# Two transformer blocks on one core: rotary turns by exchanged halves, and another order of VectorE's work in the second block

## The chip, the core and the metric

The kernel runs on one core of one Trainium2 chip. TensorE (the matrix engine, PE), VectorE (DVE), ScalarE (ACT) and GpSimd (POOL) each work through a list of instructions of their own, in order; SyncE (SP) issues the loads of weights. They wait for one another through semaphores. TensorE writes its products into PSUM, eight banks of 128 partitions by 512 float32; all else lies in SBUF. The metric is the device time of one execution in microseconds (us).

## The reference

Everything is float32, with 256 tokens ("latents") of 1024 features, and 256 context tokens in the first block.

The first block has two layers. A layer normalises and modulates its input, projects it with `w_in`, forms grouped heads (6 query heads and 2 key heads of 64 features) and latent heads (6 heads of 96 features, of which the last 32 are turned), runs attention over context and latents, adds a pooling branch, projects with `w_out`, and ends with a squared-ReLU MLP of width 4096. The second block has two layers too: a projection to 10256 features, eight heads of causal attention with two maps each, eight heads of a gated recurrence computed as a second masked product, gates, and three output projections.

The part that the change touches is the rotary turn. In the first block, for the latents only:

```python
def apply_rope(x, cos, sin):
    half = x.shape[-1] // 2
    xf = x.astype(jnp.float32)
    x1, x2 = xf[..., :half], xf[..., half:]
    return jnp.concatenate([x1 * cos - x2 * sin, x1 * sin + x2 * cos], axis=-1).astype(x.dtype)
```

and the same formula for queries and keys of the second block. It is `x * cos + swapped(x) * signed_sin`, where `swapped` exchanges the two halves of a head's features. The other touched parts are the softmax of the two maps (`softmax(where(causal, q·k * scale, -inf))`, of which the kernel computes the maximum first) and `u = sigmoid(ga) * ya + sigmoid(gb) * yb; x + u @ w_o`.

## The kernel before, in words

Activations lie with features on partitions and tokens along the free axis. Weights come from HBM in slots of 1024 x 512 (2 MB) into a ring of three. Products of the MLP and of the whole second block are "split": a weight granule (1024 x 128) is rounded by ScalarE to a high part (`hi_to`, L1516), VectorE subtracts it from the raw weight to make the low part (`lo_to`, L1926), and TensorE makes three cheap products for each of eight chunks, hi·hi, hi·lo, lo·hi (`split_product`, L1128 to L1130, 24 matmuls). In the second block three granule buffers take turns, so the granule split while product n is done serves product n + 3. All other products are plain float32 matmuls.

**Units.** Queries and keys are made unit by unit (`run_units`): 4 grouped units, 6 + 6 latent ones (`qm`, `km`) in a layer of the first block, 8 + 8 units `aq`, `ak` in a layer of the second. For each unit TensorE makes the projection, ScalarE squares it (L1475), TensorE sums the squares with a matrix of ones (`mean_squares`, L1022), ScalarE makes the reciprocal root (L1486 to L1488), VectorE corrects and applies it (L1909, L1911, L1970). Four units later TensorE multiplies the unit by a constant rotation matrix (`rotate`, L1039), VectorE multiplies that by the sine table into one of two buffers `rs` (`sine_product`, L1980), and GpSimd multiplies the unit by the cosine (L892) and adds `rs` (L895); `roped` counts the units that are done. In the second block `av`, `bif` and `bv` products follow the units, before any query is used. In the first block the four `vm` products follow, and attention begins once the grouped units are turned; it reaches the latent heads after its grouped pairs.

**Steps of the second block.** There are 32 units u of (head, block of 128 queries), the first 16 of causal attention, the last 16 of the recurrence, and 37 steps. In step s TensorE transposes the weights of unit s - 2 (L1381), every second step makes an output (L1393 to L1395, into one bank that ScalarE must have emptied, L1763), makes the scores of unit s (L1410 to L1419, into two banks that ScalarE's exponentials of unit s - 1, L1748, must have emptied) and one or two of 48 further projections (`mid_of`: `first`, and `others` in 11 of 37 steps). VectorE's order in a step: the maximum of the scores (L2200), which ScalarE's exponentials wait for; `projected` for `first`, which splits the next granule (L1926) and finishes the projection (L2170, or the three convolution taps L2154); the weights of the unit (L2217 to L2219); every second step a gate (L2185); `projected` for `others`. An output's root is due in the next step, where ScalarE scales the output by it behind its exponentials (L1763); the root of the mean square is made by GpSimd in 16 small instructions (`root_of_mean`, L952 to L960).

**Output projections.** `outa`, `outb`, `wo` have eight products each. During `outb` VectorE makes `zt` (L2240), GpSimd adds it (L984), copies the sum to its high part (L985) and subtracts it for the low part (L986); `ua_ready` counts these, and VectorE waits for it before it writes `zt` again. The first `wo` product needs all eight of them, one for each of its chunks.

## Time and profile before

| | us |
|---|---|
| median of three runs | 1970.27 (1967.19 to 1971.59) |
| the profiled execution, its own time | 1969.74 |
| its span, first to last instruction | 1967.9 |

| engine | busy us | share of the span |
|---|---|---|
| PE, matmuls | 1840.9 | 94% |
| PEld, weight loads | 1477.3 | 75% |
| DVE | 1101.7 | 56% |
| ACT | 881.7 | 45% |
| POOL | 397.6 | 20% |

Busy time is a union over instructions. Ends of matmuls are modelled, so a busy TensorE need not be at its peak. The granted clock of TensorE was 0.963 of full speed over the span. An arrow in a row (`<-ACT pb L1748`) names what ended the idle time before an instruction. A matmul with float32 operands appears as two records. Layers of the first block run from about 50 to 740 us and from 740 to 1128 us, layers of the second from 1128 to 1549 us and from 1549 us to the end.

### The profile page before, as it was taken

Reading aid. Unit: us, or ns where it says so; the run is one execution under the profiler, and the core shown is the slowest. Engines: PE = TensorE matmul, PEld = TensorE weight load, DVE = VectorE, ACT = ScalarE, POOL = GpSimd, SP = SyncE. Lnnn points to the kernel's source line nnn. Section 1 sums busy time; section 2 is a strip of 40 time slices with the busy share of each in tenths; the row PEclk is TensorE's granted clock in tenths of the full one; section 3 lists DMA queues with packets and bytes.
Section 4 is the critical chain, followed back from the end, with each engine's and each line's share of the span. In section 5 each row is a group of like instructions: output and inputs, shape, how many; then the busy total and the mean of one; then the engine's idle time right before and its main releaser. Section 6 shows DMA issues by size and latency. Waiting matters only on the chain.

```text
span 1967.9 us, 28606 instructions
## 1 busy us (share of the span) xinstructions
PE 1840.9 (94%) x10840; PEld 1477.3 (75%) x10840; DVE 1101.7 (56%) x1939; ACT 881.7 (45%) x1757; POOL 397.6 (20%) x834
## 2 busy tenths in 40 slices
PE   4999999899999998999999989988999899889998
PEld 2453454588888885547999988777899898778997
DVE  3317841687777532382555576566555575655554
ACT  2327630433332324462555565555553564555542
POOL 1014200000000000230000024055544061355433
PEclk8899989899999999999899999989999999999999
DMA  8411631244555341202455534423434325322350
GB/s 302 136 45 44 213 128 43 86 171 172 187 183 187 129 110 43 86 1 73 142 173 187 194 109 147 146 87 112 142 133 172 129 98 210 127 87 92 130 199 37
DMA packets 139875, 255.26 MB, mean 130 GB/s; under 512 B 14926, under 2 KB 21724, under 8 KB 139612
## 3 DMA queue, kind: packets, MB, share of 16 engines
q1 hardware_dynamic: 138742, 251.16, 36.6%
q8 instruction: 88, 1.44, 0.3%
q0 software_dynamic: 704, 2.10, 0.3%
q14 instruction: 47, 0.39, 0.1%
q10 hardware_dynamic: 294, 0.18, 0.0%
HBM read 252.38 MB, written 1.05 MB: 129 GB/s over the span
## 4 chain that ended last, share of the span: by engine, by line
PE 80%; DVE 8%; ACT 5%; issue 3%; POOL 1%; SPq 1%; DMA 1%; ACTq 0%; DVEq 0%; POOLq 0%
PE ps L1128 16%; PE ps L1130 15%; PE ps L1129 15%; PE ps L1137 10%; PE ps L1022 3%; PE ps L1243 2%; PE ps L1269 1%; PE ps L1039 1%; PE ps L1255 1%; PE ps L1335 1%; PE ps L1336 1%; PE ps L1337 1%; PE ps L1102 1%; SPq L803 1%; DVE big_r L1926 1%
## 5 line engine op out<-in xcount | busy, mean ns | idle before, releaser
L1926 DVE TENSOR_TENSOR big_r<-ring,big_r 128x1024 fp32r<-128x1024 f32 x198 | 245.3, 1240 | 259.4 <-ACT big_r L1516 259.0
L1516 ACT ACTIVATE big_r<-ring 128x1024 fp32r<-128x1024 f32 x198 | 209.4, 1059 | 387.7 <-PE ps L1130 379.0
L1129 PE MATMUL ps<-big_r 128*128 128x256 f32 (+1 forms) x1120 | 374.4, 334 | 0.0
L1128 PE MATMUL ps<-hT_r,big_r 128*128 128x256 f32 (+1 forms) x896 | 290.9, 325 | 10.9 <-DVE big_r L1935 10.6
L1130 PE MATMUL ps<-hT_r,big_r 128*128 128x256 f32 (+1 forms) x896 | 283.5, 316 | 0.0
L1129 PEld LDWEIGHTS ps<-big_r 128*128 128x128 f32 x1120 | 215.5, 192 | 19.3
L1137 PE MATMUL ps<-hT,ring 128*128 128x512 f32 (+2 forms) x576 | 207.2, 519 | 10.8 <-ACT hT L1537 9.2
L1128 PE MATMUL ps<-big_r 128*128 128x256 f32 (+1 forms) x592 | 195.6, 330 | 1.4 <-DVE big_r L2083 1.4
L1130 PE MATMUL ps<-big_r 128*128 128x256 f32 (+1 forms) x592 | 194.6, 329 | 0.0
L1128 PEld LDWEIGHTS ps<-hT_r,big_r 128*128 128x128 f32 x896 | 172.8, 193 | 27.5 <-issue 11.8
L1137 PEld LDWEIGHTS ps<-hT,ring 128*128 128x128 f32 (+1 forms) x576 | 109.0, 191 | 105.9 <-issue 95.0
L1130 PEld LDWEIGHTS ps<-hT_r,big_r 128*128 128x128 f32 x896 | 173.2, 193 | 10.5
L1926 DVE TENSOR_TENSOR cst_r<-ring,w_ukv_sb_r 128x1024 fp32r<-128x1024 f32 x70 | 87.3, 1248 | 114.5 <-ACT w_ukv_sb_r L1516 114.5
L1128 PEld LDWEIGHTS ps<-big_r 128*128 128x128 f32 x592 | 112.4, 190 | 11.9 <-DVE big_r L2083 2.2
L1130 PEld LDWEIGHTS ps<-big_r 128*128 128x128 f32 x592 | 112.4, 190 | 10.0
L1892 DVE SCALAR_TENSOR_TENSOR pT<-ring,csilu,pT 128x512 f32<-128x512 f32 x168 | 118.5, 747 | 1.3
L1128 PE MATMUL ps<-hT_r,w_ukv_sb_r 128*128 128x256 f32 x384 | 114.6, 298 | 0.0
L1516 ACT ACTIVATE w_ukv_sb_r<-ring 128x1024 fp32r<-128x1024 f32 x70 | 74.1, 1058 | 83.6 <-PE ps L1130 72.0
L1130 PE MATMUL ps<-hT_r,cst_r 128*128 128x256 f32 x384 | 110.0, 286 | 0.0
L1129 PE MATMUL ps<-xT_r,w_ukv_sb_r 128*128 128x256 f32 x384 | 109.8, 286 | 0.0
L907 POOL MEMSET big<- 128x1088 f32 x2 | 2.2, 1080 | 531.3 <-PE ps L1130 531.3
L1909 DVE SCALAR_TENSOR_TENSOR nt<-ps,nt 128x256 f32<-128x256 f32 (+3 forms) x74 | 39.0, 527 | 125.9 <-ACT nt L1488 125.6
(290 smaller groups left out, 4144.0 us busy)
## 6 DMA issues: line engine op xcount, KB each, us to landing
ring<-in_w_in SPq DMA_DIRECT2D x42, 2048.0 KB, 7.8
ring<-in_w_mlp SPq DMA_DIRECT2D x32, 2048.0 KB, 7.8
ring<-in_w_mod SPq DMA_DIRECT2D x24, 2048.0 KB, 8.0
ring<-in_w_out SPq DMA_DIRECT2D x4, 2048.0 KB, 8.5
ring<-in_w_out_a SPq DMA_DIRECT2D x4, 2048.0 KB, 8.6
ring<-in_w_out_b SPq DMA_DIRECT2D x4, 2048.0 KB, 8.0
ring<-in_w_o SPq DMA_DIRECT2D x4, 2048.0 KB, 8.5
ring<-in_w_in SPq DMA_DIRECT2D x12, 256.0 KB, 5.1
```

Source lines behind the costliest of these rows:

```text
L803: queue.dma_start(prow[row:row + src.shape[0], s, off:off + src.shape[1]], src).then_inc(rows_landed[s], 16)
L1022: last = mm(b[0:parts, 0:T], ones, sq[0:parts, n % SQ, 0:T], start=(j == 0), stop=(j == chunks - 1))
L1039: fill(mm(b[0:parts, 0:SEQ], rot, lat, start=True, stop=True), key)
L1128: mm(b[:, 0:T], w_hi[:, k, :], hi(k), start=(k == 0), stop=False)
L1129: mm(b[:, 0:T], w_hi[:, k, :], lo(k), start=False, stop=False)
L1130: last = mm(b[:, 0:T], w_lo[:, k, :], hi(k), start=False, stop=(k == KC - 1))
L1137: last = mm(b[0:cols, 0:T], w[:, k, m:m + cols], src(k), start=(k == 0), stop=(k == KC - 1))
L1243: fill(mm(banks[e][:, 0:tiles * P], lhs, rhs, start=True, stop=True), (tag, "s", 2 * j + e))
L1516: act_fn(hi, raw, ACT.Copy).then_inc(hi_ready, 1)
L1892: ins = V.scalar_tensor_tensor(acc, w, c, acc, ALU.mult, ALU.add)
L1909: drain(V.scalar_tensor_tensor(r2, bank(key)[0:parts, 0:T], width * EPS, r2, ALU.add, ALU.mult), key)
L1926: V.tensor_tensor(lo, raw, hi.bitcast(F32), ALU.subtract).then_inc(lo_ready, 1)
```

## The change

It has three parts.

1. The rotation products, their banks and the two rotation matrices are gone. Units are turned in four groups a layer ("turns"): 2, 2, 6 and 6 units in the first block, 4 each in the second. When the last unit of a turn is in SBUF, GpSimd issues DMAs that copy each half to the other half's partitions in a free buffer (4 DMAs, or 2 for the latent heads, whose 32 rows alone take part); GpSimd multiplies all units of the turn by the cosine in one instruction, VectorE the swapped copy by a signed sine in one instruction, and GpSimd adds them. VectorE's instruction stands two units after the turn's last one, for the fourth turn after the granules of `av` (second block) or in step 2 of attention (first block). The scores of the second block wait once for all four turns.
2. In the steps of the second block, VectorE puts the last `projected` of each step behind the next step's maximum.
3. During `outb`, GpSimd only adds; ScalarE makes the high part (`u_rounded`) and VectorE the low part (`u_rest`), and VectorE splits its granule after `zt` instead of before.

The diff, cut to its core; the removed `rope_units`, `rotate` and `sine_product` are printed above.

```diff
@@ constants
 MS_LAG = 1
-ROT_LAG = 4
+SWAP_LAG = 2
+SWAP_STEP = 2
-    put("rot64", P, rotation(P, [(0, 32), (64, 32)]))
-    put("rot96", MQK, rotation(MQK, [(MNOPE, MROPE // 2)]))
+    put("sign", P, np.where(np.arange(P) % HD < HD // 2, -1.0, 1.0)[:, None])
-    put("sing", P, np.tile(sg, (4, 1)))
+    put("sing", P, np.concatenate([-sg, sg, -sg, sg], 0))
-    put("sinm", MQK, np.concatenate([np.zeros((MNOPE, SEQ)), sm, sm], 0))
+    put("sinm", MQK, np.concatenate([np.zeros((MNOPE, SEQ)), -sm, sm], 0))
+def turns_of(tag):
+    if tag[0] == "b":
+        return [[f"a{x}{c}" for c in range(n, n + 4)] for x in "qk" for n in (0, 4)]
+    return [["q0", "q1"], ["q2", "k"], [f"qm{h}" for h in range(MH)], [f"km{h}" for h in range(MH)]]
+        def turn_of(tag, t):
+            if tag[0] == "b":
+                units = (aqT, akT)[t // 2][:, 4 * (t % 2):4 * (t % 2) + 4, :]
+                return units, pT[:, 0, :, :], cos2[:, :], sin2[:, :], slice(0, P), HD // 2
+            if t < 2:
+                units = big[:, 0:4 * TOK].rearrange("p (c t) -> p c t", c=4)[:, 2 * t:2 * t + 2, LAT:]
+                return units, rs[:, :, :], cc("cosg"), cc("sing"), slice(0, P), HD // 2
+            units = (qmT, kmT)[t - 2][:, :, LAT:]
+            free = hT[:, 3:6, :].rearrange("p c (s t) -> p (c s) t", s=2)
+            return units, free, cc("cosm"), cc("sinm"), slice(MNOPE, MQK), MROPE // 2
+        def turned(tag, t):
+            return 4 * ((DEPTH if tag[0] == "b" else 0) + tag[1]) + t + 1
@@ POOL
-            def rope_units(tag, units, part):
...
+            def turn(tag, t):
+                units, free, cos, _, rows, half = turn_of(tag, t)
+                for name in turns_of(tag)[t]:
+                    await_drained(pool, (tag, name, 0))
+                for o in range(rows.start, rows.stop, 2 * half):
+                    for to, of in ((o, o + half), (o + half, o)):
+                        pool.dma_start(free[to:to + half, :, :], units[of:of + half, :, :]).then_inc(swap_landed, 16)
+                        swaps[0] += 16
+                pool.wait_ge(swap_landed, swaps[0])
+                x = units[rows, :, :]
+                link(nc.gpsimd.tensor_tensor(x, x, cos[rows, :].unsqueeze(1).to_broadcast(list(x.shape)), ALU.mult))
+                pool.wait_ge(sine_made, turned(tag, t))
+                nc.gpsimd.tensor_tensor(x, x, free[rows, :, :], ALU.add).then_inc(roped, 1)
+                pool.wait_ge(roped, turned(tag, t))
-                rope_units(tag, units_a(i), 0)
-                rope_units(tag, units_m(i), 1)
+                for t in range(4):
+                    turn(tag, t)
-                rope_units(tag, units_b(), 0)
+                for t in range(4):
+                    turn(tag, t)
-                    link(nc.gpsimd.tensor_tensor(tgaT[:, c, :], tgaT[:, c, :], zt[:, c % 2, :], ALU.add))
-                    link(nc.gpsimd.tensor_copy(u_hi[:, c, :], tgaT[:, c, :]))
-                    nc.gpsimd.tensor_tensor(u_lo[:, c, :], tgaT[:, c, :], u_hi[:, c, :].bitcast(F32), ALU.subtract)\
-                        .then_inc(ua_ready, 1)
+                    nc.gpsimd.tensor_tensor(tgaT[:, c, :], tgaT[:, c, :], zt[:, c % 2, :], ALU.add).then_inc(u_summed, 1)
@@ TensorE
-            def rotate(tag, name):
-                for j in range(n + ROT_LAG):
+                for j in range(n + max(MS_LAG, len(tail))):
-                    if 0 <= j - ROT_LAG and is_roped(units[j - ROT_LAG][0]):
-                        rotate(tag, units[j - ROT_LAG][0])
-                pe.wait_ge(roped, roped_before(tag, 1))
+                pe.wait_ge(roped, turned(tag, 1))
-                            pe.wait_ge(roped, roped_before(tag, 1) + 2 * MH)
+                            pe.wait_ge(roped, turned(tag, 3))
                 for step in range(STEPS):
+                    if step == 0:
+                        pe.wait_ge(roped, turned(tag, 3))
-                        if p < NH2:
-                            pe.wait_ge(roped, roped_before(tag, 0) + NH2 + h + 1)
-                        else:
+                        if p >= NH2:
@@ ScalarE
+                def u_rounded(c):
+                    act.wait_ge(u_summed, 8 * l + c + 1)
+                    act_fn(u_hi[:, c, :], tgaT[:, c, :], ACT.Copy).then_inc(u_hi_ready, 1)
                     hi_to(split_by((tag, name, c)))
+                    if name == "outb" and c >= 1:
+                        u_rounded(c - 1)
+                    if name == "outb" and c == 7:
+                        u_rounded(c)
@@ VectorE
-            def sine_product(tag, name):
+            def sine_product(tag, t):
+                _, free, _, sin, rows, half = turn_of(tag, t)
+                n_swaps[0] += 16 * (rows.stop - rows.start) // half
+                dve.wait_ge(swap_landed, n_swaps[0])
+                x = free[rows, :, :]
+                V.tensor_tensor(x, x, sin[rows, :].unsqueeze(1).to_broadcast(list(x.shape)), ALU.mult)\
+                    .then_inc(sine_made, 1)
             def run_units(tag, units):
+                names = [name for name, _, _ in units]
+                at = {names.index(turn[-1]) + SWAP_LAG: t for t, turn in enumerate(turns_of(tag)[:3])}
                 for j, (name, kind, _) in enumerate(units):
...
+                    if j in at:
+                        sine_product(tag, at[j])
                 if tag[0] == "b":
                     lo_to(gran_no[("av", tag[1], 0), 3] + B_BUFS)
+                    sine_product(tag, 3)
@@ VectorE, attention of the first block
                     if j < steps:
+                        if j == SWAP_STEP:
+                            sine_product(tag, 3)
@@ VectorE, steps of the second block
+                left = []
                 for step in range(STEPS):
...
                         V.tensor_reduce(st[:, 2:4], scores, AX_X, ALU.max, negate=True).then_inc(nmax_ready, 1)
+                    for name, c in left:
+                        projected(name, c)
+                    left = (first + others)[-1:]
...
-                    for name, c in first:
+                    for name, c in (first + others)[:-1]:
                         projected(name, c)
...
-                    for name, c in others:
-                        projected(name, c)
+                for name, c in left:
+                    projected(name, c)
...
+                def u_rest(c):
+                    dve.wait_ge(u_hi_ready, 8 * l + c + 1)
+                    V.tensor_tensor(u_lo[:, c, :], tgaT[:, c, :], u_hi[:, c, :].bitcast(F32), ALU.subtract)\
+                        .then_inc(ua_ready, 1)
                 for c in range(8):
                     key = (tag, "outb", c)
                     await_bank(dve, key)
-                    lo_to(split_by(key))
-                        dve.wait_ge(ua_ready, 8 * l + c - 1)
+                        dve.wait_ge(u_summed, 8 * l + c - 1)
...
+                    lo_to(split_by(key))
+                    if c >= 1:
+                        u_rest(c - 1)
+                u_rest(7)
```

## Rows read from the trace of the kernel before

**Rows 1.** The page, the chain that ended last: shares of the span by engine.

```profile
PE 80%; DVE 8%; ACT 5%; issue 3%; POOL 1%; SPq 1%; DMA 1%; ACTq 0%; DVEq 0%; POOLq 0%
```

**Rows 2.** Stretches: length, busy PE, PEld, DVE, ACT, POOL, granted clock, DMA share, GB/s.

```profile
1256.90:1355.80 98.90, 82.58 (x643) 75.13 (x642) 60.52 (x112) 55.37 (x166) 44.39 (x108) 0.94 0.31 113
1363.00:1447.50 84.50, 84.50 (x638) 75.74 (x637) 46.32 (x117) 44.27 (x117) 41.63 (x142) 1.00 0.34 118
1670.40:1770.50 100.10, 84.30 (x644) 76.80 (x643) 60.77 (x112) 55.59 (x166) 43.56 (x108) 0.93 0.31 112
```

**Rows 3.** Timeline of TensorE, second block's units: start us, us, instruction, records.

```profile
1170.38 0.59 PE L1039 MATMUL ps<-big,cst 128*128 128x256 f32 x2
1170.81 0.38 PE L1022 MATMUL ps<-sq,cst 128*128 128x256 f32 x1
...
1174.08 0.59 PE L1039 MATMUL ps<-big,cst 128*128 128x256 f32 x2
...
1174.76 0.47 PE L1128 MATMUL ps<-hT_r 128*128 128x256 f32 x1
```

**Rows 4.** Stretches of four units (second block) and three `km` units (first).

```profile
1160.10:1175.00 14.90, 14.90 (x114) 14.48 (x113) 12.25 (x22) 10.17 (x21) 9.80 (x9) 1.00 0.41 142
170.10:180.40 10.30, 10.30 (x25) 2.68 (x24) 8.41 (x12) 7.50 (x13) 4.07 (x7) 1.00 0.01 2
```

**Rows 5.** Timelines of VectorE and GpSimd in those units of the second block.

```profile
1168.02 1.22 DVE L1926 TENSOR_TENSOR hT_r<-ring,hT_r 128x1024 fp32r<-128x1024 f32 x1 [0.31 <-ACT hT_r L1516]
1171.01 0.42 DVE L1980 TENSOR_TENSOR rs<-ps,sin 128x256 f32<-128x256 f32 x1
1171.75 1.23 DVE L1926 TENSOR_TENSOR big_r<-ring,big_r 128x1024 fp32r<-128x1024 f32 x1 [0.32 <-ACT big_r L1516]
1171.86 1.71 POOL L895 TENSOR_TENSOR big<-big,rs 128x256 f32<-128x256 f32 x1
```

**Rows 6.** Groups by line and shape of GpSimd.

```profile
L881 POOL DMA_DIRECT2D w_pool_sb<-in_w_pool x8 | 4.2, 526 | 0.0
L915 POOL TENSOR_TENSOR big<-big 128x542 f32<-128x542 f32 x2 | 2.2, 1088 | 0.0
L915 POOL TENSOR_TENSOR big<-big 128x271 f32<-128x271 f32 x2 | 1.3, 637 | 0.0
```

**Rows 7.** DMA issues: engine, number, KB each, median us to landing.

```profile
w_pool_sb<-in_w_pool POOLq DMA_DIRECT2D x8, 16.0 KB, 7.7
out<-ring SPq DMA_DIRECT2D x1, 1024.0 KB, 4.0
```

**Rows 8.** Timelines around one stall in the second block's steps.

```profile
1300.18 0.20 POOL L960 TENSOR_TENSOR rn<-rn,stat 128x2 f32<-128x2 f32 x1
1302.20 2.36 DVE L2154 SCALAR_TENSOR_TENSOR big<-sq,prm,big 128x256 f32<-128x256 f32 x3
1304.49 0.68 DVE L2200 TENSOR_REDUCE stat<-ps 128x2 f32<-128x512 f32 x1
1306.85 0.52 PE L1393 MATMUL ps<-big,pT 128*128 128x128 f32 x2 [3.89 <-ACT sq L1763]
1310.48 0.25 POOL L952 TENSOR_SCALAR rn<-rn 128x2 f32<-128x2 f32 x1
1315.78 0.44 POOL L960 TENSOR_TENSOR rn<-rn,stat 128x2 f32<-128x2 f32 x1
```

**Rows 9.** TensorE's waits, first and third stretch of Rows 2: us, times, longest.

```profile
PE ps L1393 <- ACT sq L1763: 8.7, 3, 3.9
PE ps L1410 <- ACT pb L1748: 7.1, 5, 2.8
...
PE ps L1393 <- ACT sq L1763: 8.9, 3, 3.8
```

**Rows 10.** TensorE's timeline, first `wo` product of each layer.

```profile
1519.87 0.39 PE L1128 MATMUL ps<-big_r,w_ukv_sb_r 128*128 128x256 f32 x1 [1.02 <-POOL xT_r L986]
1521.82 0.39 PE L1128 MATMUL ps<-big_r,w_ukv_sb_r 128*128 128x256 f32 x1 [1.33 <-POOL xT_r L986]
```

More of the change, by code:

```diff
@@ L75 @@
 _at = 0
-for _name, _n in (("ident", P), ("ones", P), ("ones64", P), ("rot64", P), ("rot96", MQK), ("mask", P),
+for _name, _n in (("ident", P), ("ones", P), ("ones64", P), ("mask", P), ("sign", 1),
                   ("invf", 1), ("cosg", SEQ), ("sing", SEQ), ("cosm", SEQ), ("sinm", SEQ), ("invn", 2 * SEQ)):
@@ L93, in shape_constants @@
     put("ones64", P, np.kron(np.eye(2), np.ones((64, 64))))
-    def rotation(n, blocks):
-        r = np.zeros((n, n))
-        for s, half in blocks:
-            for j in range(half):
-                r[s + half + j, s + j] = -1.0
-                r[s + j, s + half + j] = 1.0
-        return r
-    put("rot64", P, rotation(P, [(0, 32), (64, 32)]))
-    put("rot96", MQK, rotation(MQK, [(MNOPE, MROPE // 2)]))
     put("mask", P, np.where(np.arange(P)[None, :] > np.arange(P)[:, None], -1e30, 0.0))
+    put("sign", P, np.where(np.arange(P) % HD < HD // 2, -1.0, 1.0)[:, None])
     put("invf", P, (np.float32(THETA) ** (-np.arange(0, HD, 2, dtype=np.float32) / np.float32(HD)))
@@ L209, in unit_plan @@
                 ms += 1
-                if is_roped(name):
-                    take((tag, name, "rot"), 6 + rot % 2)
-                    rot += 1
     for i in range(DEPTH):
@@ L882, in _ @@
             pool.wait_ge(const_landed, 32)
-            def rope_units(tag, units, part):
-                n = roped_before(tag, part)
-                for name, kind, _ in units:
-                    if kind != "norm" or not is_roped(name):
-                        continue
-                    parts, t0, T, dsts, _, _, _, (_, cos, _) = unit_of(tag, name)
-                    lat = dsts[0] if tag[0] == "b" else dsts[0][:, LAT - t0:]
-                    await_bank(pool, (tag, name, "rot"))
-                    link(nc.gpsimd.tensor_tensor(lat, lat, cos[0:parts, :], ALU.mult))
-                    await_drained(pool, (tag, name, "rot"))
-                    nc.gpsimd.tensor_tensor(lat, lat, rs[0:parts, n % 2, :], ALU.add).then_inc(roped, 1)
-                    n += 1
+            swaps = [0]
+            def turn(tag, t):
[12 more added lines that the diff above has]
+                pool.wait_ge(roped, turned(tag, t))
             for i in range(DEPTH):
@@ L1777, in _ @@
                         projected(name, c)
-                for key in [(tag, name, c) for name in AFTER for c in range(8)]:
-                    await_bank(act, key)
-                    hi_to(split_by(key))
+                for name, c in [(name, c) for name in AFTER for c in range(8)]:
+                    await_bank(act, (tag, name, c))
+                    hi_to(split_by((tag, name, c)))
+                    if name == "outb" and c >= 1:
+                        u_rounded(c - 1)
+                    if name == "outb" and c == 7:
+                        u_rounded(c)
         @block.vector
@@ L1961, in _ @@
             nt_free = []
-            n_rot = [0]
             def apply_norm(tag, name):
-                parts, t0, T, dsts, gains, _, width, _ = unit_of(tag, name)
+                parts, t0, T, dsts, gains, _, width = unit_of(tag, name)
                 n = newton((tag, name, "ms"), parts, T, width)
@@ L1990, in run_units @@
                         apply_norm(tag, name)
-                    pend.append(name if is_roped(name) else None)
-                    if len(pend) > 2 and pend[-3]:
-                        sine_product(tag, pend[-3])
+                    if j in at:
+                        sine_product(tag, at[j])
                 if tag[0] == "b":
                     lo_to(gran_no[("av", tag[1], 0), 3] + B_BUFS)
-                for name in pend[-2:]:
-                    if name:
-                        sine_product(tag, name)
+                    sine_product(tag, 3)
             def residual(key, m, i, gate, s0):
```

55 lines of the change are left out of this document (17 added, 38 removed).

## The prediction

> **What bounds the kernel now.** I read the page's chain first. TensorE carries 80% of the path that ended last, VectorE 8%, ScalarE 5% [rows 1]: time is won where TensorE loses an instruction that it executes, a wait, or half its clock, and hardly anywhere else. So the next view is the table of stretches, set over the steps of the second block. From step 0 to step 15 of the first of its layers 98.9 us pass with TensorE busy for 82.58, at a granted clock of 0.94; the same number of steps and of projections (20) in the recurrence half take 84.5 us, without idle, at 1.00. The second layer shows 100.1 us, 84.30 busy, 0.93 [rows 2]. Here lies most of what is to be had: 16.3 + 15.8 = 32.1 us idle, and 0.06 x 98.9 + 0.07 x 100.1 = 12.9 us of clock, since the levels are 1.2 and 2.4 GHz and the mean falls after the idle times. The waits name two causes, L1410 behind ScalarE's exponentials and L1393 behind ScalarE's scaling L1763 [rows 9].
>
> In the units TensorE has no gap, so each rotation counts in full: L1039 starts at 1170.38, the next instruction at 1170.81, and the next L1039 at 1174.08, that is 0.43 us in a unit of 3.70 [rows 3].
>
> **Part 1, the turns.** Removed from TensorE: 16 rotations a layer, 64 in all, at 0.43 us.
> Second block: 32 x 0.43 = 13.8 us, if nothing else becomes late. A unit then takes 3.27 us and a turn of four 13.1. VectorE is busy for 12.25 us in four units now [rows 4]; four sine products of 0.42 go, one of 1024 columns with both inputs in SBUF comes, for which I take the 1.23 us of L1926, the same shape [rows 5]: 11.8 of 13.1, 1.3 to spare. GpSimd now has four DMA issues at 0.53 = 2.1 us [rows 6], then the landing, then two instructions of 1024 columns. Those show nowhere; 271 columns take 0.64 and 542 take 1.09 us [rows 6], so 1.66 ns a column and 1.9 us on that line; in proportion to the shorter one it would be 2.4. I take 2.0. The landing shows nowhere either: 1 MB into an idle memory landed in 4.0 us, 16 KB issued by GpSimd beside other loads in 7.7 [rows 7]. A turn moves 0.5 MB; between weight loads that take 0.41 of the DMA engines [rows 4] I take the 4.0, nearest in size, and keep both ends. Then the swap is there 6.1 us after the turn's last unit, and VectorE asks for it two units on, 6.5 us: just in time. GpSimd's turn is 2.1 + 4.0 + 2 x 2.0 = 10.1 of 13.1 us, so turns don't queue up. At 7.7 VectorE waits 3.3 us.
> By the Trainium skill ("DMA: Bandwidth & Descriptors", Anatomy of one DMA) a DMA from GpSimd costs about 2.0 us plus bytes over 436 GB/s; an estimate by that page is 3.2 us for the turn, earlier than the value I use, and no row here shows such a copy.
> What hides a delay of VectorE: the granule split at 1168.02 to 1169.24 is used at 1174.76 [rows 5, 3], a lead of 5.5 us, 4.7 once two rotations less lie between. Queued behind the waiting sine product are the next units' newton steps and granules.
> A new cost is the shared access to SBUF. GpSimd's L895 starts 0.11 us behind VectorE's L1926 (1171.75, 1.23 us) and takes 1.71 us [rows 5], though 271 columns take it 0.64 [rows 6]: it ran only when VectorE was through. Now GpSimd's instructions are the long ones: two of 2.0 us a turn, each of which can hold a granule's subtraction. Bounds 0 and 4 us a turn; I take 2 us, 0.7 over the 1.3 to spare, so about 2 us a layer at most once the lead is eaten, 1 us taken. **Gain 12 us.**
> The Trainium skill ("SBUF — State Buffer", Who interferes with whom) says that the port pair goes to one of them for a whole instruction, and that two SBUF inputs on VectorE suffice for it; by that rule the trace agrees, and with splitting costing nothing the sum would be 1 or 2 us better.
> First block: 32 rotations. Eight lie among the `vm` products, where TensorE waits for VectorE anyway: 24 x 0.43 = 10.3 us. Behind the last `km` unit VectorE loses sine products and gains one of 1536 columns (1.8 us, twice, one of them in attention's step 2); GpSimd's of 1536 columns take 2.7 us on the same line, and VectorE, busy for 8.41 of 10.3 us in three `km` units [rows 4], has 0.6 us a unit to make that good. Bounds -4 to +4 us for both layers; I take -0.3. Attention's grouped pairs don't need the latent turns; these end some 12 us after the last unit, before the six steps of grouped pairs do. **Gain 10 us.**
>
> **Part 2, the maximum ahead.** One stall shows it all. VectorE is in L2154 from 1302.20, makes the maximum L2200 only at 1304.49, ScalarE's exponentials and then L1763 follow, and L1393 starts at 1306.85 after 3.89 us idle. GpSimd's root had been ready since 1300.38 [rows 8]: the maximum was late, not the root, though the wait reads L1763. With the maximum in front it starts with the scores, a granule (1.23) and sometimes a convolution (2.36 there) earlier, and the exponentials end within TensorE's projection of 24 x 0.12 = 2.9 us. So the L1410 waits go (7.1 us here, about as much in the next layer), and the L1393 waits as far as the maximum caused them (8.7 + 8.9) [rows 9].
> What is late next is the root's chain. An output starts at 1306.85; GpSimd begins at 1310.48 (its queue held a silu) and ends at 1316.22 [rows 8]; with L1763's 0.6 the next output can start 10.0 us on. TensorE's two steps take 84.5 / 15 x 2 = 11.3 us on average [rows 2] with 2.7 projections, but 9.4 with two; there 0.6 us stays idle, in about three pairs a layer, more when GpSimd is held by a granule. I leave a third of the L1393 waits. The new wait: behind the maximum stands the deferred granule. It waits for scores that TensorE makes right after the product whose bank frees that granule, at most 1.9 us, against two projections (5.7 us) until it is needed: hidden. For the recurrence half the order is the same but for the gate: nothing.
> Sum: 14 + 2/3 x 17.6 + 2/3 x 12.9 (clock, as the idle times that it follows go) = **34 us**; bounds 18 and 45.
>
> **Part 3, the rounding shared.** In the first `wo` product TensorE waits 1.02 and 1.33 us for GpSimd's last chunks [rows 10]; the other layer has somewhat more, and both a half-clock stretch behind. Afterwards the last chunk needs `zt`, an add (0.73), a copy on ScalarE behind its granule (1.06), a subtraction on VectorE behind its granule: about 3.3 us after the last `outb` product, 1.7 us earlier than now. ScalarE and VectorE have room in a product of 2.8 us (1.5 and 2.1). 2 x 1.7 + 1.6 of clock = **5 us**, bounds 2 and 10.
>
> Sum against the profiled execution, 1969.7 us: 12 + 10 + 34 + 5 = 61, **1909 us**. That execution stands 0.5 us under the median of three runs.
>
> **Rivals.**
> A. The swap is late or GpSimd's long instructions hold VectorE: landing 7.7, 3.3 us waited in three turns a layer, and 4 us a turn blocked. Against the lead of 4.7 and 1.3 a turn that leaves TensorE idle for most of what the rotations gave in the second block (12) and half in the first (5), with some 4 us of clock: 1930. For it: L895's 1.71, and 7.7. Against: the 7.7 belong to small copies queued behind larger ones of the same engine.
> B. The root's chain takes the place of the maximum and the steps win only half, 17: 1926. For it: 10.0 against 9.4 us; against: in the stall shown the root had been ready for 4.1 us when the maximum began [rows 8], and the recurrence half shows the same chain with no idle at all [rows 2].
> C. Slower. GpSimd cannot issue while VectorE holds the port: each issue waits a granule, 4 x (0.53 + 1.23) = 7.0, plus 7.7 to land, and a turn is 14.7 + 4.0 = 18.7 us against 13.1. The third sine product comes 19 us late; less 4.7 and 3 x 1.3 that is 11 us a layer, 22. In the first block two latent turns each come 5 us late in both layers, 20. Clock at 0.4 us per idle us, as in the stretches (12.9 / 32.1), 17; half of GpSimd's 16 x 2.2 us in VectorE's way, 17. Together 76 on 1909: 1985. It decides from a turn of 13.1 us on, and beats the gains from a loss of 61. Against: issues at 0.53 are short, the engine is idle between.
> The Trainium skill ("SBUF — State Buffer", SBUF: two separate sides) warns that GpSimd cannot write descriptors while VectorE is in a 2-port mode; VectorE's instructions here are mostly of two inputs, at one column a cycle, and no issue in this trace lies beside one, so it raises C's chance only a little.
> D. All idle time and clock of the named places come back: 45 + 13.8 + 12 + 8 = 79, 1891.
>
> **Chances.** Forecast 0.42 (1899 to 1919), A 0.20, B 0.20, D 0.10, C 0.06, and 0.02 that gains and losses meet. The range takes in D, A and B: 1890 to 1942. A measurement of this kernel tells 0.2% (4 us) from nothing: faster 0.92, same 0.02, slower 0.06.
>
> **What would show it.** Right: in the steps of causal attention no wait of L1410, L2200 within 0.1 us of the scores, granted clock 0.98 or more, the stretch at 80 to 84 us; a unit of 3.3 us in the second block; sine products of 1.2 us with at most 0.5 idle in front; no wait on GpSimd in the first `wo` product. Wrong: TensorE waiting for L1926 in the units, GpSimd's turn above 13 us, VectorE idle for the swap by 3 us (A, C), or L1393 waiting for L1763 right behind L960 (B).

## The result and the profile after

The changed kernel is slower by 0.3%: 1974.7 us median (1969.4 to 1983.9, 20 runs) against 1970.3 (1967.2 to 1972.4, 20 runs), ratio 1.0028, 95% interval 1.0018 to 1.0037. The forecast was 1909, its range 1890 to 1942. The profiled execution took 1975.4 us, its span is 1973.5. Line numbers have moved: the granule's L1926 is L1922 in the kernel after, the steps of the root L1909, L1911 and L1970 are L1905, L1907 and L1965, TensorE's L1022, L1128 and L1393 are L1021, L1116 and L1383, and ScalarE's L1763 is L1755; the kernels of the experiments move them again by a few lines. The page of after, engines and chain:

```profile
PE 1826.4 (93%) x10712; PEld 1457.1 (74%) x10712; DVE 1138.9 (58%) x1907; ACT 888.4 (45%) x1773; POOL 374.7 (19%) x762
...
PE 77%; DVE 9%; ACT 4%; DMA 3%; POOL 3%; issue 2%; SPq 1%; ACTq 0%; DVEq 0%; POOLq 0%
PE ps L1116 16%; PE ps L1118 15%; PE ps L1117 15%; PE ps L1125 10%; PE ps L1021 3%; DMA pT<-big 2%; PE ps L1231 2%; PE ps L1257 1%; DVE rstd L1907 1%; PE ps L1243 1%; DVE big_r L1922 1%; PE ps L1090 1%; PE ps L1323 1%; SPq L801 1%; PE ps L1324 1%
```

Compared with [rows 1], DMA and GpSimd have gone from 1% to 3% of the path each, and the path names the swap (`DMA pT<-big`) and VectorE's L1907 and L1922. TensorE is busy for 14.5 us less and the span is 5.6 us longer. To see where, I cut both traces at the same points of the work (the first score, the first product of a kind) and compared the lengths:

| stretch, us | before | after | difference |
|---|---|---|---|
| start to the end of the first block | 1129.2 | 1135.3 | +6.1 |
| units, two layers | 61.1, 60.4 | 71.7, 71.5 | +21.7 |
| `av`, then to step 0 | 56.1, 54.5 | 60.6, 61.4 | +11.4 |
| steps 0 to 16 | 106.1, 106.7 | 90.5, 92.0 | -30.3 |
| steps 16 to 31 | 84.8, 84.8 | 87.6, 87.6 | +5.6 |
| step 31 to the next layer, to the output | 96.7, 98.4 | 93.3, 93.2 | -8.6 |

The turns cost 39 us where 22 were to be won; parts 2 and 3 win 33 where 39 were forecast. Stretches of after (columns as in [rows 2]); the first and third answer to the first and third there, the second to its second, the fourth is the units, the last the output projections:

```profile
1278.20:1360.50 82.30, 77.26 (x642) 70.99 (x641) 59.24 (x111) 55.74 (x166) 46.13 (x104) 1.00 0.36 126
1368.70:1456.30 87.60, 87.60 (x638) 78.61 (x638) 46.01 (x114) 44.17 (x116) 40.74 (x143) 0.96 0.33 116
1693.20:1777.00 83.80, 78.81 (x642) 72.30 (x641) 59.55 (x111) 55.96 (x166) 46.41 (x104) 0.98 0.36 126
1146.00:1217.60 71.60, 61.77 (x414) 58.23 (x415) 54.26 (x75) 42.55 (x83) 21.64 (x17) 0.86 0.40 119
...
1456.30:1549.60 93.30, 91.92 (x771) 90.91 (x769) 52.13 (x76) 39.56 (x64) 19.89 (x48) 1.00 0.52 185
```

The units of before, for the fourth:

```profile
1139.80:1200.80 61.00, 61.00 (x438) 58.67 (x439) 48.36 (x84) 40.62 (x80) 26.79 (x22) 0.94 0.33 113
```

In the units TensorE now idles for 9.8 us and its mean granted clock is 0.86 instead of 0.94. Two turns show why. GpSimd in the second block's units (start, duration, instruction, idle before and who ended it):

```profile
1179.33 3.42 POOL L894 TENSOR_TENSOR big<-big,cos 128x1024 f32<-128x1024 f32 x1 [6.75 <-DMA pT<-big]
1182.83 3.21 POOL L896 TENSOR_TENSOR big<-big,pT 128x1024 f32<-128x1024 f32 x1
...
1209.83 2.00 POOL L890 DMA_DIRECT2D pT<-big  x4 [3.83 <-DVE big L1965]
1214.33 2.37 POOL L894 TENSOR_TENSOR big<-big,cos 128x1024 f32<-128x1024 f32 x1 [2.50 <-DMA pT<-big]
```

VectorE, an undisturbed unit first, then beside GpSimd's first two instructions above, last beside the L894 at 1214.33:

```profile
1171.81 0.42 DVE L1905 SCALAR_TENSOR_TENSOR nt<-ps,nt 128x256 f32<-128x256 f32 x1 [0.31 <-ACT nt L1476]
...
1172.72 0.48 DVE L1965 SCALAR_TENSOR_TENSOR big<-ps,prm,rstd 128x256 f32<-128x256 f32 x1
...
1179.28 1.23 DVE L1975 TENSOR_TENSOR pT<-pT,sin 128x1024 f32<-128x1024 f32 x1 [2.76 <-DMA pT<-big]
1180.42 3.42 DVE L1922 TENSOR_TENSOR big_r<-ring,big_r 128x1024 fp32r<-128x1024 f32 x1
...
1184.20 2.12 DVE L1907 SCALAR_TENSOR_TENSOR rstd<-nt,rstd 128x256 f32<-128x256 f32 x1
1186.36 0.48 DVE L1965 SCALAR_TENSOR_TENSOR big<-ps,prm,rstd 128x256 f32<-128x256 f32 x1
...
1215.22 1.75 DVE L1907 SCALAR_TENSOR_TENSOR rstd<-nt,rstd 128x256 f32<-128x256 f32 x1
```

TensorE in the same stretch:

```profile
1175.51 0.59 PE L1021 MATMUL ps<-sq,cst 128*128 128x256 f32 x2
1175.75 0.47 PE L1116 MATMUL ps<-hT_r,w_ukv_sb_r 128*128 128x256 f32 x1
...
1184.22 1.22 PE L1021 MATMUL ps<-sq,cst 128*128 128x256 f32 x2 [1.99 <-DVE nt L1905]
1186.89 0.58 PE L1116 MATMUL ps<-hT_r,big_r 128*128 128x256 f32 x1 [1.45 <-DVE big L1965]
```

Three delays follow one another. VectorE waits 2.76 us for the swap. Its granule L1922 then takes 3.42 us instead of 1.22, beside L894, which had begun 1.1 us before it. L1907, 0.42 us undisturbed, takes 2.12 beside L896. The ends of the rows show the two engines taking turns, instruction by instruction: L1975 ends at 1180.51, L894 2.24 us later, L1922 1.09 us after that, L896 2.20 us after L1922, L1907 0.28 us after L896. So each duration is a wait for the other engine's instruction and then its own time, and GpSimd's own time is 2.2 us, not 3.4. Not every instruction is held: L1905, which takes one of its inputs from PSUM, took 0.41 us at 1183.76, in the middle of L896. At 1214.33 L894 got in with hardly a wait, took 2.37 us, and it was L1907 that waited (1.75). TensorE idles for 3.4 us in the first of these turns, and the products behind run at half the clock (L1021 takes 1.22 us for its 0.59; granted clock 0.50 from 1187 to 1190).

The first block shows the same: GpSimd, then VectorE with its 96-row units, then GpSimd, VectorE and TensorE in attention, where the instruction that is held is the scaling of the attention weights, L2039:

```profile
170.11 2.90 POOL L894 TENSOR_TENSOR big<-big,cst 32x1536 f32<-32x1536 f32 x1 [2.33 <-DMA hT<-big]
176.26 3.42 POOL L896 TENSOR_TENSOR big<-big,hT 32x1536 f32<-32x1536 f32 x1 [3.25 <-DVE hT L1975]
```

```profile
170.61 2.95 DVE L1907 SCALAR_TENSOR_TENSOR rstd<-nt,rstd 96x512 f32<-96x512 f32 x1
...
176.88 3.36 DVE L1907 SCALAR_TENSOR_TENSOR rstd<-nt,rstd 96x512 f32<-96x512 f32 x1
181.65 0.69 DVE L1907 SCALAR_TENSOR_TENSOR rstd<-nt,rstd 96x512 f32<-96x512 f32 x1
```

```profile
192.72 2.90 POOL L894 TENSOR_TENSOR big<-big,cst 32x1536 f32<-32x1536 f32 x1 [2.36 <-DMA hT<-big]
198.16 3.41 POOL L896 TENSOR_TENSOR big<-big,hT 32x1536 f32<-32x1536 f32 x1 [2.54 <-DVE hT L1975]
```

```profile
192.71 3.06 DVE L2039 TENSOR_SCALAR pb<-pb,stat 128x256 f32<-128x256 f32 x1
195.88 0.35 DVE L2039 TENSOR_SCALAR pb<-pb,stat 128x256 f32<-128x256 f32 x1
199.56 2.15 DVE L2039 TENSOR_SCALAR pb<-pb,stat 128x256 f32<-128x256 f32 x1
```

```profile
201.87 0.66 PE L1243 MATMUL ps<-cst,pb 128*128 128x128 f32 x2 [4.02 <-DVE pb L2039]
```

### The profile page after: what moved, and what is told of

It reads as the page before. It is cut to its first block, busy times and chain, and to the rows that moved or that the text cites. A ratio compares the mean times of both kernels' runs of the same rounds, so it can differ in the third digit from the quotient of the medians.

```text
span 1973.5 us, 28119 instructions
## 1 busy us (share of the span) xinstructions
PE 1826.4 (93%) x10712; PEld 1457.1 (74%) x10712; DVE 1138.9 (58%) x1907; ACT 888.4 (45%) x1773; POOL 374.7 (19%) x762
## 4 chain that ended last, share of the span: by engine, by line
PE 77%; DVE 9%; ACT 4%; DMA 3%; POOL 3%; issue 2%; SPq 1%; ACTq 0%; DVEq 0%; POOLq 0%
PE ps L1116 16%; PE ps L1118 15%; PE ps L1117 15%; PE ps L1125 10%; PE ps L1021 3%; DMA pT<-big 2%; PE ps L1231 2%; PE ps L1257 1%; DVE rstd L1907 1%; PE ps L1243 1%; DVE big_r L1922 1%; PE ps L1090 1%; PE ps L1323 1%; SPq L801 1%; PE ps L1324 1%
## 5 line engine op out<-in xcount | busy, mean ns | idle before, releaser
L1922 DVE TENSOR_TENSOR big_r<-ring,big_r 128x1024 fp32r<-128x1024 f32 x198 | 252.4, 1275 | 234.7 <-ACT big_r L1504 234.7
L1116 PE MATMUL ps<-hT_r,big_r 128*128 128x256 f32 (+1 forms) x896 | 293.7, 328 | 16.5 <-DVE big_r L1931 12.8
L1116 PEld LDWEIGHTS ps<-hT_r,big_r 128*128 128x128 f32 x896 | 176.3, 197 | 33.4 <-issue 11.8
L1116 PE MATMUL ps<-big_r 128*128 128x256 f32 (+1 forms) x592 | 195.6, 330 | 1.4 <-DVE big_r L2078 1.4
L1125 PEld LDWEIGHTS ps<-hT,ring 128*128 128x128 f32 (+1 forms) x576 | 108.4, 190 | 106.7 <-issue 96.0
L1118 PEld LDWEIGHTS ps<-hT_r,big_r 128*128 128x128 f32 x896 | 176.5, 197 | 10.2
L1922 DVE TENSOR_TENSOR cst_r<-ring,w_ukv_sb_r 128x1024 fp32r<-128x1024 f32 x70 | 95.0, 1357 | 81.4 <-ACT w_ukv_sb_r L1504 81.4
L1905 DVE SCALAR_TENSOR_TENSOR nt<-ps,nt 128x256 f32<-128x256 f32 (+3 forms) x74 | 38.9, 526 | 152.2 <-ACT nt L1476 151.5
L1116 PEld LDWEIGHTS ps<-big_r 128*128 128x128 f32 x592 | 112.5, 190 | 11.9 <-DVE big_r L2078 2.2
L1116 PE MATMUL ps<-hT_r,w_ukv_sb_r 128*128 128x256 f32 x384 | 114.2, 297 | 3.3 <-DVE big L1965 3.3
L1021 PE MATMUL ps<-sq,cst 128*128 128x256 f32 (+3 forms) x236 | 90.2, 494 | 19.3 <-DVE nt L1905 9.9
```

Of the source, the lines that this page charges most:

```text
L1021: last = mm(b[0:parts, 0:T], ones, sq[0:parts, n % SQ, 0:T], start=(j == 0), stop=(j == chunks - 1))
L1116: mm(b[:, 0:T], w_hi[:, k, :], hi(k), start=(k == 0), stop=False)
L1118: last = mm(b[:, 0:T], w_lo[:, k, :], hi(k), start=False, stop=(k == KC - 1))
L1125: last = mm(b[0:cols, 0:T], w[:, k, m:m + cols], src(k), start=(k == 0), stop=(k == KC - 1))
L1905: drain(V.scalar_tensor_tensor(r2, bank(key)[0:parts, 0:T], width * EPS, r2, ALU.add, ALU.mult), key)
L1922: V.tensor_tensor(lo, raw, hi.bitcast(F32), ALU.subtract).then_inc(lo_ready, 1)
```

## Experiments

Each kernel ran 4 times beside 7 runs of the kernel before. Ratios are to the kernel before, with their 95% interval.

**1. The parts one by one.** `turns_only` is the kernel before with part 1, `ahead_only` with part 2, `rest_only` with parts 2 and 3; the edits are those of the diff above.

> The kernel before with part 1 alone. Theory L: the first block loses 6 us and the units, av and the wait at step 0 of the second block 33 us, as in the changed kernel, so 1970 + 39 = 2009 us. Rival S: the turns delay the start of the steps but the steps then run with less idle time, so that a part comes back: 1990 us.

> The kernel before with parts 2 and 3 of the change alone (maximum ahead, rounding shared); the rotation products stay. Theory L (the turns lost time by themselves, and parts 2 and 3 won it): the stretches of the steps and of the output projections moved by -24.7 and -8.6 us in the changed kernel, so this one takes 1970 - 33 = 1937 us, with the units at 61 us as before. Rival S (the gain of the steps was borrowed: the turns delayed the start of the steps, so that granules and loads of weights were further ahead when they began): step 0 to 16 wins less than half of its 15 us, and the time is 1950 or more.

> The kernel before with part 2 alone. By the stretches steps 0 to 31 won 24.7 us in the changed kernel and the output projections 8.6: so 1970 - 25 = 1945 us, and part 3 is worth 7 (1938.7 for both). Forecast in the prediction: 34 for part 2 and 5 for part 3, that is 1936 here. Rival: the two hang together (the output projections also win by the order of the granules at the end of the steps), 1940.

| kernel | us | ratio |
|---|---|---|
| part 1 | 2010.2 | 1.020 (1.0171 to 1.0230) |
| part 2 | 1947.8 | 0.9888 (0.9873 to 0.9904) |
| parts 2 and 3 | 1938.7 | 0.9840 (0.9822 to 0.9858) |

Theory L holds, rival S falls: the turns lose 38 us by themselves, and with rotation products in front of them steps 0 to 31 still win 22.5 of the 24.7 us. Part 2 is worth 23 us, part 3 another 9, the difference of two ratios that are each uncertain by 3 to 4 us. In what follows 1938.7 is the mark that a kernel with turns must beat.

**2. GpSimd's instructions in unit pieces** (`cut`).

```diff
-link(tensor_tensor(x, x, cos[...].to_broadcast(...), mult))      # all units of the turn
+for k in range(n): tensor_tensor(units[rows, k, :], units[rows, k, :], cos[rows, :], mult)
-tensor_tensor(x, x, free[rows, :, :], add)
+for k in range(n): tensor_tensor(units[rows, k, :], units[rows, k, :], free[rows, k, :], add)
```

> The changed kernel with GpSimd's two instructions of a turn cut into one for each unit (4 x 256 columns in the second block, 6 x 256 rows-by-columns for the latent heads), all else the same. Theory P (a long GpSimd instruction holds VectorE for its whole length): VectorE waits for at most one piece of some 0.8 us at a time, L1922 and L1907 in the units fall from 3.4 and 2.1 us to at most 2 and 1.2, the units of the second block go from 71.6 to about 65 us a layer and attention in the first block back to its 95.6 and 45.7: together 1975 - 2 x 6 - 10 = 1953 us. Rival Q (what counts is the late swap, 6.9 us to land against 4.0): the pieces change nothing in the wait for the swap, and the time stays at 1970 to 1978.

1953.1 us, 0.9910 (0.9893 to 0.9927). GpSimd and VectorE in one turn:

```profile
1168.83 5.99 POOL L896 TENSOR_TENSOR big<-big,cos 128x256 f32<-128x256 f32 x4 [6.79 <-DMA pT<-big]
1174.90 3.37 POOL L901 TENSOR_TENSOR big<-big,pT 128x256 f32<-128x256 f32 x3
1178.35 1.59 POOL L904 TENSOR_TENSOR big<-big,pT 128x256 f32<-128x256 f32 x1
```

```profile
1169.92 1.76 DVE L1930 TENSOR_TENSOR big_r<-ring,big_r 128x1024 fp32r<-128x1024 f32 x1
...
1172.99 1.23 DVE L1930 TENSOR_TENSOR cst_r<-ring,w_ukv_sb_r 128x1024 fp32r<-128x1024 f32 x1
```

Theory P holds: the same columns cost VectorE 0.5 us instead of 2.2 in a granule, and the units take 61.3 us in the first layer and 63.2 in the second. Now GpSimd is the one that waits: four pieces of the cosine product take 5.99 us, that is 1.5 each, and a turn of 2.0 + 6.8 + 6.0 + 3.4 + 1.6 = 19.8 us doesn't fit into 13.1. Its last turn holds `av` up (31.4 and 29.0 us against 24.4). That the sum 1953 was met is luck: the units won 18.6 us, not 12, and steps 0 to 16 took 93.8 us in both layers instead of the 90.5 and 92.0 of the changed kernel.

**3. GpSimd's work left out** (`no_pool`): product and sum on 8 columns.

```diff
-x = units[rows, :, :]
+x = units[rows, 0, 0:8]
```

> The changed kernel with GpSimd's cosine product and its sum on 8 columns of one unit only; the rest of both is left out, so queries and keys are hardly turned. Swaps, sine products and all waits stay. Theory P: the units take 60 us or less instead of 71.6, av 24.4, attention in the first block 95 and 45: 1975 - 2 x (12 + 6) - 10 = 1929 us or below. Rival Q (the late swap): VectorE still waits 2.5 to 7 us in front of the sine products, the units stay at 68 us or more, and the time is 1960 or more.

1928.9 us, 0.9781 (0.9759 to 0.9803): GpSimd's two instructions cost 45.8 us, more than the 39 that the turns lost. But the units take 61.3 and 62.0 us, as with rotation products, not the 60 or less of theory P. The first layer:

```profile
1132.90:1194.20 61.30, 57.24 (x414) 54.13 (x415) 44.81 (x74) 41.14 (x80) 10.55 (x16) 0.94 0.46 138
```

VectorE there still waits for the swap:

```profile
1183.12 1.23 DVE L1975 TENSOR_TENSOR pT<-pT,sin 128x1024 f32<-128x1024 f32 x1 [5.71 <-DMA pT<-big]
```

**4. The wait for the swap taken away as well** (`no_pool_lag`): `SWAP_LAG` 4 instead of 2.

> The kernel with GpSimd's products and sums left out but for 8 columns (1928.9 us), with VectorE's sine product four units behind a turn's last unit instead of two (the first three turns of a layer). It takes the wait for the swap away too: there the units of the second block still take 61.3 and 62.0 us, as with rotation products, though 16 of these are gone. Theory Q2 (what is missing there is the late swap): the units fall to 61.3 - 16 x 0.43 = 54.4 us and the first block's by 1 or 2: 1928.9 - 2 x 7 - 2 = 1913 us. Rival V (VectorE's own sine products of 1024 columns and the clock keep it): 60 us a layer, 1925 or more.

1932.3 us, 0.9806 (0.9789 to 0.9823), which can't be told from the 1928.9 of experiment 3: theory Q2 is right about the units and wrong about the whole. They fall to 56.3 and 57.2 us (from 61.3 and 62.0, together -9.8):

```profile
1135.60:1191.90 56.30, 55.79 (x415) 53.88 (x415) 45.66 (x74) 41.05 (x80) 8.46 (x16) 0.95 0.48 151
```

and the wait comes back behind them. The fourth swap is issued after the last unit, VectorE waits for it with `av`'s granules behind, and TensorE waits for one of those:

```profile
1210.23 1.23 DVE L1975 TENSOR_TENSOR pT<-pT,sin 128x1024 f32<-128x1024 f32 x1 [6.94 <-DMA pT<-big]
```

`av` takes 28.0 and 26.5 us instead of 23.9 and 24.6 (+6.0), the first block 2.6 more, the rest 4.

**5. Why the swap lands late** (`no_load`). In the changed kernel the times from the last issue to GpSimd's product are 7.2, 7.9, 3.0, 7.7 us in the first layer and 7.6, 7.7, 3.4, 8.3 in the second; during the short ones the weights being loaded are the 0.5 MB of `bif`, during the others 2 MB. The times count from the start of the last of the four issues.

```diff
+elif key[0] in ("ak", "av", "bif", "bv") and key[1] == 0:
+    sp.nop().then_inc(slot_landed[r], 16)
```

> The kernel with GpSimd's products and sums left out but for 8 columns (1928.9 us), that also leaves out the loads of the weights of ak, av, bif and bv in the first layer of the second block (stale weights are used there); the second layer is as before and serves as the control. Theory W (the swap of 0.5 MB lands late because it shares the DMA engines with a 2 MB load): its landing, 7 to 8 us behind the last issue beside such a load and 3.0 to 3.6 beside the load of 0.5 MB, falls to 2 to 3 us in all four turns of the first layer, VectorE does not wait for it any more, and the layer's units go from 61.3 to 55 or 56 us; the second layer keeps its 7 to 8 us and 62 us. Theory G (it is GpSimd's way of issuing): the landings of the first layer stay at 7 us. The whole: 1923 us with W, 1929 with G.

1924.8 us, 0.9778 (0.9758 to 0.9799). One turn in the layer without the loads (GpSimd), then one in the control layer:

```profile
1156.69 2.01 POOL L892 DMA_DIRECT2D pT<-big  x4 [294.73 <-DVE big L1967]
1161.06 0.20 POOL L896 TENSOR_TENSOR big<-big,cos 128x8 f32<-128x8 f32 x1 [2.36 <-DMA pT<-big]
...
1553.26 2.05 POOL L892 DMA_DIRECT2D pT<-big  x4 [57.86 <-DVE big L1967]
1561.97 1.24 POOL L896 TENSOR_TENSOR big<-big,cos 128x8 f32<-128x8 f32 x1 [6.66 <-DMA pT<-big]
```

Theory W holds: 2.85, 2.9, 2.85, 2.9 us without the loads, 7.2, 7.6, 3.9, 7.9 with them. The units take 56.1 us without the loads; the control layer takes 59.9 where 62 was expected, so some 2 of the 5.2 us to 61.3 need not come from the loads. By the Trainium skill ("DMA: Bandwidth & Descriptors", Anatomy of one DMA) a DMA issued by GpSimd takes about 2.0 us plus bytes over 436 GB/s, for the 0.5 MB of the turn 3.2 us by my estimate; without loads the trace comes within 0.4 us of that (2.9), beside a load of 2 MB it does not (7.2 to 7.9).

**6. The swap issued by ScalarE** (`act_swap`; `act_swap_cut` on the kernel of experiment 2).

```diff
-pool.dma_start(free[to:to + half, :, :], units[of:of + half, :, :])    # GpSimd
+act.wait_ge(roped, turned(tag, t) - 1)
+act.dma_start(free[to:to + half, :, :], units[of:of + half, :, :])     # ScalarE, two units on
```

> The changed kernel with the swap's DMAs issued by ScalarE instead of GpSimd: in the second unit after a turn's last one, between the square and the reciprocal root; the fourth turn of the second block right behind the units. GpSimd's long instructions stay. Theory G (the swap lands late, 6.9 us, because GpSimd issues it): from ScalarE it lands within 4 us, VectorE no longer waits 2.5 to 7 us in front of the sine products, and the units and av of the second block lose 5 us a layer less: 1975 - 10 = 1965 us. Rival W (it lands late because the DMA engines are busy with the loads of weights): 6 to 7 us from ScalarE too, nothing is won, 1975 or more, as four issues stand in ScalarE's queue.

> The same edit on the kernel with GpSimd's instructions in unit pieces (1953.1 us). Theory G: 1953 - 12 = 1941 us; the wait of 4.75 us for the low part in av goes, as GpSimd's turn ends earlier. Rival W: 1953 or more. Against 1938.7 us of the kernel without turns it tells whether turns can be had for less than the rotations they replace.

1982.1 us, 1.0065 (1.0050 to 1.0081), and 1957.9 us, 0.9937 (0.9921 to 0.9954): both lose, by 7.4 and 4.8 us. The median landing is shorter (5.0 and 3.7 us against 6.9), but fewer of the turns now run wholly beside a load of 2 MB. Issues and landings in `act_swap`, the second turn of the first layer, beside such a load, then its fourth, with none under way:

```profile
ring<-in_w_in SPq DMA_DIRECT2D x1, 2048.0 KB, 11.1
pT<-big ACTq DMA_DIRECT2D x4, 128.0 KB, 7.0
...
pT<-big ACTq DMA_DIRECT2D x4, 128.0 KB, 2.3
```

ScalarE in `act_swap`, then in `act_swap_cut`:

```profile
1177.70 1.97 ACTq L1530 DMA_DIRECT2D pT<-big  x3
1179.77 0.47 ACT L1469 ACTIVATE rstd<-ps,epsc 128x256 f32<-128x256 f32 x1 [2.27 <-issue]
```

```profile
1182.46 2.44 ACTq L1538 DMA_DIRECT2D pT<-big  x4
1185.00 0.47 ACT L1477 ACTIVATE rstd<-ps,epsc 128x256 f32<-128x256 f32 x1 [8.42 <-issue]
```

Four issues hold ScalarE 2.3 us (the first of `act_swap` runs beside its square), and in the second kernel it waits 6 us before them for GpSimd's sum, which frees the buffer. Theory G falls here too, and W holds: in `act_swap` the swap lands 7.3 to 7.7 us behind its last issue in the four turns beside a load of 2 MB, 3.3 to 3.5 in the two beside the load of `bif`, and 2.3 to 2.4 in the two without a load, whichever engine issues it.

**7. What is left of the waits in the steps** (`root_one`, `silu_behind`, on `rest_only`).

```diff
-for _ in range(3):        # Newton iterations of root_of_mean
+for _ in range(1):
```

> The kernel with parts 2 and 3 alone (1938.7 us), GpSimd's root with one Newton iteration instead of three: eight of 16 small instructions are left out, 8 x 0.28 = 2.2 us, and the roots are less exact. Theory R (what is left of the waits of L1383 for L1755 in causal attention, 1.3 + 3.2 + 0.5 + 3.3 = 8.2 us a layer, is the root's chain on GpSimd): the waits shrink to about 1 + 1 us, steps 0 to 16 go from 93.2 to about 85, and the time is 1938.7 - 2 x 7 = 1925 us. Rival M (the maximum is still late): the waits stay, 1937 to 1939.

```diff
 root_of_mean(p)
+while behind: silu(behind.pop(0))
...
-silu(late)
+behind.append(late) if (the next step has a root) else silu(late)
```

> The kernel with parts 2 and 3 alone (1938.7 us), with GpSimd's silu of a step that has no root put behind the next step's root. Nothing is left out. Theory R2 (the root's chain is late because a silu of 2 to 2.5 us stands in front of it in GpSimd's queue): the two long waits of 3.2 us a layer lose 2 us each, clock with them: 1938.7 - 10 = 1929 us. Rival: the silu itself, now later, holds up the tanh that wants its buffer back or the gate behind it, and the time is 1938 or more.

1915.0 us, 0.9722 (0.9707 to 0.9736), and 1932.0 us, 0.9810 (0.9792 to 0.9827). GpSimd in `rest_only`, ahead of a wait of 3.17 us that ends at 1310.67:

```profile
1302.29 1.59 POOL L946 TENSOR_TENSOR big<-big,w_ukv_sb 128x256 f32<-128x256 f32 x1
...
1309.76 0.20 POOL L962 TENSOR_TENSOR rn<-rn,stat 128x2 f32<-128x2 f32 x1
```

TensorE's waits from step 0 to 16, `rest_only` first, then `root_one`:

```profile
PE ps L1392 <- ACT sq L1766: 8.2, 4, 3.3
```

```profile
PE ps L1392 <- ACT sq L1766: 0.4, 1, 0.4
```

Theory R holds and its price was low: steps 0 to 16 go from 94.0 and 92.5 us to 82.1 and 82.2 with the clock at 1.00, steps 16 to 31 from 86.7 to 84.8, and the whole wins 23.7 us instead of 14. Moving the silu wins 6.7 us (forecast 10); its interval touches that of `rest_only`, but steps 0 to 16 show it too: 90.7 and 90.6 us, 5.2 less.

**8. A version to keep** (`root_two`): `silu_behind` with two Newton iterations.

> A version meant to be kept: parts 2 and 3 without the turns, the silu behind the root, and two Newton iterations instead of three (the seed's error of 3 per cent goes to some 5 in a million, against one in a thousand after one). Four small instructions of 0.28 us go from each root. Theory R (the root's chain): each of the four waits of 1.3 to 2.3 us a layer loses 1.1 us, and clock with it: 1932.0 - 2 x 5 = 1922 us. If silu order and iterations give the same time back only once, 1926.

1916.8 us, 0.9731 (0.9717 to 0.9746): 2.7% faster than the kernel before and 2.9% faster than the changed one. Leaving out the third iteration wins 15 us on `silu_behind` where 10 were forecast, and the time is within 2 us of `root_one`: what the order of the silu and the iterations give doesn't add up. One wait of 1.5 us is left in the first layer's steps, shown here up to step 15:

```profile
1254.60:1332.30 77.70, 76.12 (x633) 70.01 (x633) 60.66 (x111) 55.86 (x165) 39.52 (x83) 1.00 0.37 131
```

## Why the prediction was wrong

The forecast was 61 us; what came is a loss of 4.4. By its terms:

| term | forecast | stretches | alone |
|---|---|---|---|
| turns, second block | -12 | +33 | |
| turns, first block | -10 | +6 | |
| turns, both | -22 | +39 | +38 (part 1) |
| maximum ahead | -34 | -25 | -23 (part 2) |
| rounding shared | -5 | -9 | -9 (parts 2 and 3 less part 2) |

**The turns: the step that failed is "What hides a delay of VectorE".** It took the granule's lead, 4.7 us, although it saw the newton steps (VectorE's corrections of the root) queued behind the same wait. TensorE's waits in the units name these: L1021 waits for L1905 and L1116 for L1965, which free the bank of the mean squares and the bank of the unit. Only in `av`, behind the units, does it wait for a granule (3.4 us). Undisturbed, L1905 starts at 1171.81 and the L1021 that needs its bank at 1175.51; L1965 starts at 1172.72 and the product behind it at 1175.75. These leads are 3.3 and 2.5 us to the end of the instruction. Against them stood two delays, each at the bad end of its bounds:
- the landing, taken at 4.0 us of the range 4.0 to 7.7, was 7.2 to 8.3 in three of four turns (6.8 to 7.8 counted as the prediction did, from the end of the issues). [rows 7] showed both ends; the nearer in size was chosen, but its 1 MB went into an idle memory, as the prediction itself says, and what decides is the load beside (experiments 5 and 6). The swap came 9.3 us after the turn's last unit, not 6.1.
- the blocking, taken at 2 us a turn of 0 to 4, was 3.9 (2.2 in L1922, 1.7 in L1907). The size of GpSimd's instruction, 2.0, was nearly right: its own time is 2.2 us, and the rest of the 3.2 to 3.4 is its wait for VectorE. What was missed is where the hold falls: on the next instruction of VectorE that works in SBUF alone, a granule or L1907, and behind it stand L1905 and L1965 with their short leads. The Trainium skill ("GPSIMD Engine Reference", 3.1 Elementwise) has 2.6 cycles an element for an instruction with two inputs, by which I estimate 2.2 us for 1024 of them at the 1.2 GHz of its examples; the trace agrees, with 2.20 to 2.24 us behind VectorE's end and 2.37 for the row that hardly waited.

VectorE was busy for 54.26 of 71.6 us, so there was room on the mean. It was the length of one hold, in the wrong place, that hurt: experiment 2 moves the same columns in shorter pieces and wins 21.6 of the 45.8 us that GpSimd's work costs (experiment 3).

**Rival A had the mechanism and the inputs, 7.7 and 4 us, and still said 1930.** It set them against the lead of 4.7 us, let a turn lose no more than its rotations gave, and priced the clock at 4 us. In the first layer's units TensorE idles for 9.8 us, and the mean clock falls by 0.08, which is 5.7 of 71.6 us in that stretch alone. Rival C, at 1985, was near in size for the turns, with another mechanism: GpSimd's issues took 0.51 us each and none was blocked. The condition that it set did come true, a turn longer than 13.1 us (2.0 + 6.8 + 3.4 + 3.2 = 15.4), but the turns did not pile up as it said: the units had become slower too, and GpSimd sat idle for 3.8 us before it issued the next one.

**First block: "-4 to +4 us"** left out what a hold does there. The turn of `qm` holds two of VectorE's newton steps for 2.3 and 2.7 us (2.95 and 3.36 against 0.69) in the `km` units, where VectorE had 0.6 us a unit to spare; TensorE's waits for VectorE from 165 to 190 us go from 2.5 to 5.3 us. The turn of `km` falls into attention, and there it is the scaling L2039 that is held, 3.06 and 2.15 us against 0.35: TensorE waits for it once for 4.0 us, at a granted clock of 0.77 from 200 to 215 us where it had 1.00. Attention went from 95.6 to 100.9 us and from 45.7 to 50.1, 9.7 us together; the rest of the first block won 3.6 of the 10 forecast.

**Part 2 was right for the maximum, wrong for "two thirds of the L1393 waits".** Steps 0 to 15 take 82.3 and 83.8 us (forecast 80 to 84), no wait of the scores is left, the clock is 1.00 and 0.98. Of the waits for the scaling, 8.7 and 8.9 us in the two layers [rows 9], 8.3 stayed in each, longest 3.3: the wait was put down to the maximum because that was last in the stall of [rows 8]; with it out of the way the root was, in GpSimd's queue behind a silu (experiment 7). That was rival B at half its price: it took 17 us from this part, and 9 to 11 were missing. The last of these waits stands at step 16, and the recurrence half, 84.8 us before and 87.6 now, starts at half clock behind it (0.55 in its first 7.3 us, which is 3.3 us).

**Part 3 was right**, with the clock undercounted: no wait on GpSimd is left in the first `wo` product (0.7 us for VectorE's part is), and the clock of the output projections is 1.00 instead of 0.98 and 0.97.

Even with GpSimd's work and the loads of one layer left out the turns win 14 us on 1938.7 (1924.8), of the 22 forecast. What stays open is where the other 8 us went, and how a whole turn could be had without these losses. A second buffer for the swap, or the fourth turn's swap split so that it lands before `av`, were not tried.

## What to carry to other kernels

Before work moves to another engine, find the shortest lead that its delay would eat, which is that of the first buffer or bank to run out, not that of the instruction one has in mind; and compare it with the longest single hold, not with mean busy time. Take the landing of a small copy from a row beside the same bulk loads. When a wait has two causes that end close together, removing the later one wins only the distance between them.

## What the runs showed of the hardware

GpSimd and VectorE took turns by whole instructions where both worked in SBUF: VectorE's granule took 3.42 us for its 1.22 and its L2039 3.06 for its 0.35 beside GpSimd, while L1905, with an input from PSUM, kept its 0.41. A GpSimd instruction of hardly any length takes as long as VectorE's that began just before it: 8 columns took 1.24 us beside VectorE's sine product and 0.20 us without it (experiment 5). With GpSimd in pieces of 256 columns VectorE lost little (1.23 to 1.76 us a granule), while each piece of GpSimd's cosine product took 1.5 us and of its sum 1.1 to 1.6. A copy of 0.5 MB inside SBUF landed 2.9 us after its last issue alone and 7 to 8 us beside a load of 2 MB, and issued by ScalarE 2.3 to 2.4 and 7.3 to 7.7 us. Four DMA issues cost ScalarE 2.3 to 2.4 us of its own time, and GpSimd 2.0.
